# A fused mLSTM, windowed attention and mixture-of-experts layer: when a short second half signals, which engine squares, and how the last expert is ordered

## The reference, cut to what matters

```python
S, D, NE, F = 1024, 1024, 16, 512       # tokens, width, experts, expert width
hn = rmsnorm(x, norm_mix)
z = hn @ w_in + b_in                    # 1024 x 2824
hm = mlstm(conv+silu(z_q, z_k), z_v, gates)   # 4 heads, chunks of 64
ha = sliding_window_attention(...)      # 8 heads, window 128, sinks, T5 bias
x = x + concat(hm, ha) @ w_out
xt = rmsnorm(x, norm_ffn)
g = argmax(xt @ w_grp + b_grp)          # top-1 of 4 groups
e = top2(xt @ w_er + b_er inside g)     # top-2 of the group's 4 experts
for e in range(16):                     # each token goes to 2 experts
    y += combine[:, e] * ((silu(xt @ w_gate[e]) * (xt @ w_up[e])) @ w_down[e])
out = rmsnorm(x + y, norm_final)
```

## Time and profile before

| | |
|---|---|
| median of three runs | 963.27 us (963.26 to 966.44) |
| the profiled execution | 963.42 us, its span 961.6 us |
| PE busy | 915.7 us, 95% of the span |
| DVE busy | 663.6 us, 69% |
| ACT busy | 457.4 us, 48% |
| POOL busy | 294.6 us, 31% |
| mean granted clock of TensorE | 0.978 |

### The profile page before, as it was taken

How to read it: one execution, slowest core, us unless ns; L and a number is a source line. 1 busy time by engine, 2 the same in 40 slices (tenths; PEclk the granted TensorE clock), 3 DMA queues, 4 the chain that set the end, 5 groups by cost and what they waited for, 6 DMA issues and landing times.

```text
span 961.6 us, 16200 instructions
## 1 busy us (share of the span) xinstructions
PE 915.7 (95%) x4984; PEld 762.4 (79%) x4985; DVE 663.6 (69%) x1145; ACT 457.4 (48%) x721; POOL 294.6 (31%) x307
## 2 busy tenths in 40 slices
PE   8899999999999899999989999999999999999886
PEld 7688788888888778888887777787887787788674
DVE  6683457575665887767788887775575776687756
ACT  7433425253443533222135776564545665575653
POOL 1300000000000010001016888354354665594524
PEclk9999999999999999999978999999999999999998
DMA  8531103021202752112648999987678796989775
GB/s 301 148 87 44 44 22 110 23 69 42 67 22 92 214 199 88 66 66 98 231 179 302 354 377 368 327 262 221 221 237 250 257 359 243 326 275 339 221 249 235
DMA packets 86199, 183.56 MB, mean 191 GB/s; under 512 B 8395, under 2 KB 29216, under 8 KB 86146
## 3 DMA queue, kind: packets, MB, share of 16 engines
q1 hardware_dynamic: 76114, 153.48, 45.6%
q0 software_dynamic: 9872, 29.32, 11.5%
q10 hardware_dynamic: 160, 0.07, 0.0%
HBM read 150.89 MB, written 31.40 MB: 190 GB/s over the span
## 4 chain that ended last, share of the span: by engine, by line
PE 83%; DVE 7%; ACT 4%; issue 3%; POOL 1%; DMA 1%; DVEq 0%; ACTq 0%; POOLq 0%; SPq 0%
PE PS L1885 20%; PE PS L1887 20%; PE PS L1886 19%; PE PS L2203 2%; PE PS L2178 2%; PE PS L2205 2%; PE PS L2153 2%; PE PS L2230 1%; PE PS L2231 1%; PE PS L2237 1%; DVE WP L590 1%; ACT junk L951 1%; PE PS L2018 1%; PE PS L2138 1%; PE PS L1992 1%
## 5 line engine op out<-in xcount | busy, mean ns | idle before, releaser
L1641 DVE TENSOR_TENSOR WL<-RAW,WH 128x2048 fp32r<-128x2048 f32 x94 | 214.0, 2290 | 48.4 <-ACT WH L1064 45.5
L1064 ACT ACTIVATE WH<-RAW 128x2048 fp32r<-128x2048 f32 x96 | 183.8, 1914 | 28.2 <-PE PS L1887 18.4
L1885 PE MATMUL PS<-WH,XH 128*128 128x512 f32 x304 | 124.5, 409 | 8.0 <-DVE YB L1816 6.0
L1887 PE MATMUL PS<-WH,XL 128*128 128x512 f32 x304 | 119.8, 394 | 0.0
L1886 PE MATMUL PS<-WL,XH 128*128 128x512 f32 x304 | 119.4, 393 | 0.0
L804 POOL TENSOR_TENSOR dst<-dst,stat 128x4 f32<-128x4 f32 x8 | 8.1, 1018 | 328.1 <-DVE dst L1602 328.1
L812 POOL TENSOR_TENSOR stat<-stat 128x1 f32<-128x1 f32 x107 | 73.1, 695 | 69.4 <-ACT YB L1174 51.1
L1885 PE MATMUL PS<-HNH,WP 128*128 128x512 f32 x208 | 84.2, 405 | 1.6 <-issue 1.6
L1887 PE MATMUL PS<-HNH,WP 128*128 128x512 f32 x208 | 81.9, 394 | 0.0
L1886 PE MATMUL PS<-HNL,WP 128*128 128x512 f32 x208 | 81.7, 393 | 0.0
L1885 PEld LDWEIGHTS PS<-WH,XH 128*128 128x128 f32 x304 | 57.4, 189 | 21.4 <-issue 11.0
(11 more groups left out here) (386 smaller groups left out, 2071.3 us busy)
## 6 DMA issues: line engine op xcount, KB each, us to landing
RAW<-in_w_gate_dram SPq DMA_DIRECT2D x32, 1024.0 KB
RAW<-in_w_up_dram SPq DMA_DIRECT2D x32, 1024.0 KB
RAW<-in_w_down_dram SPq DMA_DIRECT2D x32, 1024.0 KB
wraw<-in_w_in_dram SPq DMA_DIRECT2D x22, 512.0 KB, 4.3
XT<-in_x_dram SPq DMA_DIRECT2D x8, 512.0 KB, 7.0
vo_dram<-vo SPq DMA_DIRECT2D x16, 256.0 KB, 2.1
wout<-in_w_out_dram SPq DMA_DIRECT2D x4, 1024.0 KB, 8.0
VM<-vo_dram SPq DMA_DIRECT2D x16, 256.0 KB, 5.9
```

What stands on the lines that cost most here:

```text
L1064: A(WH[:, d % SPLITS, :], RAW[:, j, :], ACT.Copy).then_inc(s_whi, 1)
L1641: V.tensor_tensor(WLS[d % SPLITS][:, :], RAW[:, TURN[d][1] if d else 0, :], WH[:, d % SPLITS, :].bitcast(fp32), ALU.subtract).then_inc(s_w ...
L1885: mm(bank, ah, bh, start=start, stop=False)
L1887: return mm(bank, al, bh, start=False, stop=stop)
```

## The change

- Sums of squares: ACT does tiles 0 to 4 (`SQ_ACT = 5`), DVE does 5 to 7 behind its split of weight group 0, into a scratch tile of its own. POOL waits for both.
- The 14 matmuls on constants are gone; `keep_busy(9)` becomes `keep_busy(6)`. Two DVE instructions on `idle_` become one copy: the last unit's code is no longer doubled.
- `s_dn1` is incremented by the last matmul of piece 5's second half; a unit with none increments it by an instruction of PE's queue.
- The last unit takes the few path in all engines for gate, up and hidden products (not for down). `add_rows` stands behind down piece 4. POOL's drain moves one unit ahead.

```diff
+SQ_ACT = 5
+        junk_dve = at("junk_dve", aq_at + 8 * KB, [P, D])
+        s_ssq_dve, SSQ_DVE = s_set, 3
...
-            pool.wait_ge(s_ssq, NT)
+            pool.wait_ge(s_ssq, SQ_ACT)
+            pool.wait_ge(s_ssq_dve, SSQ_DVE + NT - SQ_ACT)
...
+                if not more:
+                    pool.drain()
                 pool.wait_ge(s_hb, 2 * u + 2)
...
-            pool.drain()
             for c in range(NT + 2):
...
-            for i in range(NT):
+            for i in range(SQ_ACT):
                 act.wait_ge(s_xin[i], 16)
...
             u = n_loop + 1          # ACT
-            act.wait_ge(s_wused, 6 * u + 3 + SPLITS)
-            for hf in (1, 0):
-                A(SG[:, hf, :], PS[:, 2 * hf, :], ACT.Tanh, scale=0.5).then_inc(s_th, 1)
+            def both_tanh():
+                act.wait_ge(s_wused, 6 * u + 3 + SPLITS)
+                for hf in (1, 0):
+                    gate_tanh(hf).then_inc(s_th, 1)
+            second = has_second(u)
+            with act.If(second > 1):
+                both_tanh()
+            with act.If(second < 1):
+                both_tanh()
+            with act.If(second > 0):
+                with act.If(second < 2):
+                    act.wait_ge(s_wused, 6 * u + 3 + SPLITS)
+                    low_rows(2).then_inc(s_glo, 1)
+                    gate_tanh(0).then_inc(s_th, 1)
+                    act.wait_ge(s_gsum, 2 * u + GSUM + 1)
+                    A(SG[0:FEW, 1, :], HB[0:FEW, 1, :], ACT.Tanh, scale=0.5).then_inc(s_th, 1)
+                    act.wait_ge(s_wused, 6 * u + 4 + SPLITS)
+                    low_rows(3).then_inc(s_glo, 1)
             def square(c, tile):
...
             hi_piece(u, 5)
...
             group_lo(dve, 0)
+            for i in range(SQ_ACT, NT):
+                dve.wait_ge(s_xin[i], 16)
+                if i > SQ_ACT:
+                    dve.wait_ge(s_ssq_dve, SSQ_DVE + i - SQ_ACT)
+                V.scalar_tensor_tensor(junk_dve[:, :], XT[:, i, :], 1.0, XT[:, i, :], ALU.mult, ALU.mult,
+                                       accum_out=stat[:, i:i + 1]).then_inc(s_ssq_dve, 1)
...
-            link(V.tensor_scalar(idle_[:, :], C("u"), counts[:, 3 * NU:], -1.0, ALU.subtract, ALU.is_ge))
-            link(V.scalar_tensor_tensor(tab[:, NU:2 * NU], idle_[:, :], 1.0, counts[:, NU:2 * NU], ALU.add, ALU.mult))
+            V.tensor_copy(tab[:, NU:2 * NU], counts[:, NU:2 * NU])
...
             # DVE, the last unit; both_silu and both_times_up hold the code of before
+            with dve.If(second > 0):
+                with dve.If(second < 2):
+                    dve.wait_ge(s_glo, 2 * u + GLO + 1)
+                    both_rows(HB[0:FEW, 1, :], 2).then_inc(s_gsum, 1)
+                    dve.wait_ge(s_th, 2 * u + 1)
+                    silu(0).then_inc(s_sil, 1)
+                    dve.wait_ge(s_th, 2 * u + 2)
+                    dve.wait_ge(s_gsum, 2 * u + GSUM + 1)
+                    V.scalar_tensor_tensor(HB[0:FEW, 1, :], SG[0:FEW, 1, :], 1.0, HB[0:FEW, 1, :],
+                                           ALU.add, ALU.mult).then_inc(s_sil, 1)
             last_lo_piece(u, 5)
...
+            with dve.If(second > 0):
+                with dve.If(second < 2):
+                    dve.wait_ge(s_sil, 2 * u + 2)
+                    dve.wait_ge(s_glo, 2 * u + GLO + 2)
+                    both_rows(SG[0:FEW, 1, :], 3).then_inc(s_gsum, 1)
+                    dve.wait_ge(s_gate, 32 * u + 32)
+                    dve.wait_ge(s_gsum, 2 * u + GSUM + 2)
+                    V.scalar_tensor_tensor(HB[0:FEW, 1, :], HB[0:FEW, 1, :], gt[0:FEW, 1:2], SG[0:FEW, 1, :],
+                                           ALU.mult, ALU.mult).then_inc(s_hb, 1)
+                    times_up(0, 1).then_inc(s_hb, 1)
             hidden_lo(u, 0, 1)
             hidden_lo(u, 1, 0)
             last_lo_piece(u, 6)
...
-            for _ in range(14):
-                mm(PS[:, 5, 0:P], ones[:, :], ident, start=True, stop=True)
             rank(EARLY, NT - EARLY, 3)
...
                 with pe.If(second > 0):
-                    second_down(5, 0, second)
-                down(5, 0, 0, 0).then_inc(s_dn1, 1)
+                    second_down(5, 0, second, 1)
+                with pe.If(second < 1):
+                    nc.tensor.sem_inc(s_dn1, 1)
+                down(5, 0, 0, 0)
                 down(5, 0, 0, 1).then_inc(s_wused, 1)
...
-            keep_busy(9)
+            keep_busy(6)
...
             for j, slot in ((1, 1), (2, 2), (3, 0)):     # the last unit
                 pe.wait_ge(s_wlo, 6 * u + j + 1)
-                with pe.If(second > 0):
-                    gate_up(par, j, slot, 1)
+                second_gate_up(par, j, slot, second)
                 gate_up(par, j, slot, 0).then_inc(s_wused, 1)
...
             last_hidden(u, 0, 1)
             last_hidden(u, 1, 0)
+            # down piece 4 (second half, first half) stands here now
             pe.wait_ge(s_gath[0], 16 * n_loop + 64 - FEWER[0])
             # add_rows(1), add_rows(0)
-            # down piece 4 stood here
```

More of the change, by code:

```diff
@@ L1838, in _, with both_silu @@
             u = n_loop + 1
[L1839 to L1842, removed]
[L1843 to L1849 removed]
+            def both_silu():
+                for n, hf in enumerate((1, 0)):
+                    dve.wait_ge(s_th, 2 * u + n + 1)
+                    silu(hf).then_inc(s_sil, 1)
@@ new lines, in both_times_up @@
+            def both_times_up():
+                dve.wait_ge(s_sil, 2 * u + 2)
+                dve.wait_ge(s_gate, 32 * u + 32)
+                dve.wait_ge(s_wused, 6 * u + 4 + SPLITS)
+                for hf, bank in ((1, 3), (0, 1)):
+                    times_up(hf, bank).then_inc(s_hb, 1)
+            second = has_second(u)
+            with dve.If(second > 1):
+                both_silu()
+            with dve.If(second < 1):
+                both_silu()
+            with dve.If(second > 0):
[8 more added lines that the diff above has]
+                                           ALU.add, ALU.mult).then_inc(s_sil, 1)
@@ L2218, in down, with second_down @@
                 return last
-            def second_down(j, slot, full):
+            def second_down(j, slot, full, done=0):
                 with pe.If(full > 1):
                     down(j, slot, 1, 0)
-                    down(j, slot, 1, 1)
+                    last = down(j, slot, 1, 1)
+                    if done:
+                        last.then_inc(s_dn1, done)
                 with pe.If(full < 2):
@@ L2230, in second_down @@
                             mm(down_bank(1, half), both_parts, WH[:, slot, w], start=(f == 0), stop=False)
-                            mm(down_bank(1, half), both_parts, WLS[slot][:, w], start=False, stop=(f == 3))
+                            last = mm(down_bank(1, half), both_parts, WLS[slot][:, w], start=False, stop=(f == 3))
+                    if done:
+                        last.then_inc(s_dn1, done)
             def hidden_transposes(u, n, hf, done=1):
@@ L2329, in add_rows @@
                 for half in range(2):
-                    mm(down_bank(hf, half), ident, rows_[:, hf, 512 * half:512 * half + 512], start=True, stop=alone)
+                    mm(down_bank(hf, half), ident, rows_[:, hf, 512 * half:512 * half + 512],
+                       start=alone, stop=alone)
             last_hidden(u, 0, 1)
             last_hidden(u, 1, 0)
+            pe.wait_ge(s_wlo, 6 * u + 5)
+            pe.wait_ge(s_hlo, 2 * u + 1)
+            with pe.If(second > 0):
+                down(4, 2, 1, 0)
+                down(4, 2, 1, 1)
+            pe.wait_ge(s_ye, 2 * u + 2)
+            pe.wait_ge(s_hlo, 2 * u + 2)
+            down(4, 2, 0, 0)
+            down(4, 2, 0, 1).then_inc(s_wused, 1)
             pe.wait_ge(s_gath[0], 16 * n_loop + 64 - FEWER[0])
```

15 lines of the change are left out of this document (6 added, 9 removed).

## The result

The changed kernel took 954.55 us (median of four, 953.5 to 955.57) against 964.62 beside it on the same chip (four, 963.26 to 966.44): a ratio of 0.9894, 95% interval 0.987 to 0.9919. That is 10.1 us faster, where 14.8 were forecast, and 1.55 us above the forecast's range. The profiled execution took 953.94 us (span 951.7, mean granted clock 0.970 after 0.978).

The account below looks back on a forecast made before the run. PE was taken as the bound, holding 83% of the chain that ended last, so gains come from its stream or waits. 963.42 - 4.6 - 2.0 - 8.2 + 0 gave 948.6 us; range 945.5 to 953.

Parts of the forecast that it names:

- Part 1: Start: sharing squares with DVE removes PE's 2.9 us wait and runs four products at full clock: -4.6 us.
- The rule of the Trainium skill: DVE scalar-tensor-tensor with two non-bf16 SBUF sources halves throughput; rival of half-speed squares: 952.2 us, chance 0.10.
- Part 2: Routing: fewer matmuls on constants let DVE's rank start earlier and x parts move 2.5 us: -2.0 us in sum.
- what was feared: Routing: with 17 fewer matmuls on constants, the clock can stay low for longer; 0.5 us more taken.
- Part 3: Experts: second half's down products signal 1.37 us earlier, shortening six waits for DVE's addition: -8.2 us.
- Full units wait for ACT's copy alone, hidden: Experts, full units: ACT's copy is hidden by the 6 matmuls behind it, so the earlier signal gives 0.
- Part 4: Last unit: fewer matmuls save 3.63 us, but later hidden rows and half clock eat it: 0, bounds -1.5 and +3.
- T': End of the last unit's last up product in the changed kernel; forecast at 929.3 us.
- the last scatter absorbs 0.9: End: PE ends 0.9 us later, but the last scatter, starting behind the first one, absorbs all of it.
- The second rival: End: the last unit's order costs more than the matmuls save: +3 us, 951.6 us, chance 0.13.
- Moved into POOL's idle time in unit 14 it costs nothing: End: POOL's drain, blamed for a 1.9 us late answer, costs nothing once moved into unit 14.
- three stated signs of error: Waits on line 1816 over 1 us, squares over 2 us, or PE ending more than 26 us after T'.

Follow-up runs that it names:

- e16: The changed kernel again, word for word, as base for a later set: 953.45 us, ratio 0.9859 to the kernel before.
- e4: Kernel before with only the 14 matmuls on constants taken out and keep_busy(9) cut to 6: 965.37 us, ratio 0.9993.
- e2: Kernel before with only the earlier signal of the second half's down products: 958.16 us, ratio 0.9913.
- e5: The changed kernel again, as base on another chip than its first measurement: 953.83 us, ratio 0.986 to the kernel before.
- e8: Changed kernel with add_rows ahead of the first down piece and the drain back at its old place: 952.75 us, ratio 0.9864 to before.
- e7: Changed kernel with add_rows ahead of the first down piece, drain left in unit 14: 956.38 us, ratio 0.9897 to before.
- e9: Changed kernel without POOL's drain at either place: 957.78 us, ratio 0.9922 to the kernel before.
- e13: Changed kernel with hidden rows made earlier, 16 matmuls on constants behind the last up product, drain at about 34 us: 953.55 us, ratio 0.9866 to before.
- e11: e10 plus 16 matmuls on constants behind the last up product: 955.2 us, ratio 0.9885 to the kernel before.
- e10: Changed kernel with ACT's and DVE's last-unit work reordered, add_rows first and no drain: 956.85 us, ratio 0.99 to the kernel before.

## Why the prediction was wrong, point by point

| step | forecast | measured |
|---|---|---|
| 1 squares | -4.6 | -4.5 |
| clock at 78 us | none | +1.5 (none in e16) |
| 2 routing | -2.0 | -1.7 in the profile; -0.7 (-3.6 to +2.3) in e4, by the ratio |
| 3 earlier signal | -8.2 | -9.1 (e2's units 0 to 14) |
| 4 last unit and drain | 0 | +3.3 |
| x's loads | none | +0.6 |

- **Part 1 was right to 0.1 us**: squares of 1.23, POOL at 26.6, the wait gone, the four products in 1.88 us. The rule of the Trainium skill weighed there (Vector Engine (DVE) Microarchitecture Reference, Points that are easy to get wrong) does not hold for this form: float32, two SBUF sources and a sum took 1.23 us, where half throughput was estimated at 2.35. The 1.5 us at 78 us are no price of the squares: the same kernel had them in two of three profiles (e5, but not e16). Missing was an allowance for this chance: I had priced the clock only where I removed a wait.
- **Part 2** was right up to `tab` (DVE right behind its line, the last step on `tab` 1.8 us earlier for 1.9 forecast) and wrong behind it: the parts of x moved by 1.55 us, not 2.5, since DVE stood 0.83 us waiting for ACT's part behind PE's transposes, which took 1.11 us at half clock (0.66 before). The clock did what was feared: half from 485 to 508 instead of in parts. It cost less than the 0.5 us allowed.
- **Part 3** was right for the few units (7.9 us of 8.2). "Full units wait for ACT's copy alone, hidden" was wrong: units 6 and 7 gave 1.4 us together. Their idle time stood in the view of waits under "issue", not under the addition, and I had looked at the addition alone.
- **Part 4 failed, the largest miss.** The forecast had the down work at T' + 8.2 and PE's end at T' + 24.7. It came at 9.25 and 26.8. Three terms: the down work came 1.05 us later, 0.2 of it because the hidden rows were complete at T' + 7.1 for 6.9, the rest behind PE's eight transposes, which were themselves at half clock (1.97 us, 1.31 before; 0.50 in 922 to 924) with ACT's and DVE's steps hanging on them; the half clock cost the 24 products behind it 3.05 us instead of 2.0 (8.5 us for 5.4); and "the last scatter absorbs 0.9" was no slack at all. In the earlier trace rows the second scatter starts 0.89 us after DVE's last product ended; after the change, with nothing queued ahead of it, it starts 0.84 after. I took a fixed distance for a queue.
- **How the time came to lie outside the range.** The second rival (the last unit's order costs more than the matmuls save, 0.13) had its mechanism, a longer stretch at half clock; its +3 was near the +3.3. Part 4 alone gives 948.6 + 3.3 = 951.9 us, inside the range; the 1.5 us at 78 us, 0.6 for x's loads and 0.4 in parts 1 and 2, less the 0.9 that part 3 gave beyond its forecast, and 0.4 more outside the span, take it to 953.9. So that the time fell outside the range is in part the chance of the clock.
- **"Moved into POOL's idle time in unit 14 it costs nothing"** was wrong in mechanism, though it hid in this kernel. The row shows POOL idle for 12.86 us with "issue" as the reason, which I read as 1.9 us of delay. It is the drain's own length: 12.5 to 13.2 us from the last transfer's issue in all twelve profiles that show it (in e8 DVE's variance came later still). In unit 14 it holds back the last gathers by 4.4 us (e7 against e8; 3.9 in the changed kernel against e9), which e7 turns into a wait of PE.
- **Why the order ate the gain**: my account (copy behind T, high part, low part, addition) is what the profile shows. e13 shows its price: with the queues in the right order and the idle time covered, PE's end comes 6.5 us sooner than in e5, 5.0 sooner than in e16, of which 3.0 are the clock's by e11 against e10. The order with the rows first and no drain, e10, gave 2.6 and 1.0 us, so the clock's share is the larger.

Of the three stated signs of error one came in: PE ended more than 26 us behind T'. The waits on DVE's addition were gone, and the squares took 1.23 us.

## What to carry to other kernels

A short path that makes one operand late turns its saving into idle time: list what each engine has queued ahead of the late operand, and put the work that waits for nothing first. Where an idle time of several microseconds can't be avoided, try matmuls on constants in it, and price it at the half clock that follows otherwise, about 3 us here; they kept the full clock in two of four kernels. And when a row says that an engine idled with no releaser, ask which instruction that the profile does not show stood there, before moving it.

## What the runs showed of the hardware that was not expected

- GpSimd's drain ended 12.5 to 13.2 us after the issue of the transfer before it, wherever it stood late in the program. Without one, or with one only at 34 us, the span ended 8.4 us behind GpSimd's last issue instead of 2.7 to 3.0. That what the indirect transfers leave has to be cleared before the program may end is argued from these numbers, not seen; how it grows with their number wasn't tried.
- Whether a stretch falls to 1.2 GHz can differ between executions of one kernel: 78 to 82 us at 0.57 in the changed kernel and e5, at 1.00 in e16. Whole executions of the kernel before differed by 12.8 us, between mean granted clocks of 0.985 and 0.972.
- A DVE product with a sum over two float32 sources in SBUF, 128x1024, took 1.22 to 1.23 us and 0.08 to 0.09 for the read of the sum; ACT's square took 1.06 and 0.19.
